# Order-2 Hyena convolution: the imaginary part of the spectrum products moved to GpSimd, VectorE's steps turned by one spectrum

## The chip, the cores and the metric

The kernel runs on one core of a Trainium2 chip. A core has five engines that run their own instruction streams and meet only at semaphores: TensorE (PE in the profile), VectorE (DVE), ScalarE (ACT), GpSimd (POOL) and SyncE (SP), which here only issues DMAs. They share an on-chip memory, SBUF, and the matmul accumulators, PSUM. The metric is the device time of one execution in microseconds.

## The reference

One layer of a diffusion backbone on 1024 tokens of width 1024, float32. The part that matters here is the Hyena branch: three streams v, x1, x2 of 512 channels, and twice a long convolution of the running stream with a filter, done as a product of spectra, followed by a gate.

```python
y = v.astype(jnp.float32)
for o, gate in enumerate((x1, x2)):
    yf = jnp.fft.rfft(y, n=2 * L, axis=1)
    y = jnp.fft.irfft(yf * kf[:, o], n=2 * L, axis=1)[:, :L] + hyena_bias[o].astype(jnp.float32) * y
    y = gate.astype(jnp.float32) * y
```

`yf * kf` is a complex product: real part xr*kr - xi*ki, imaginary part xr*ki + xi*kr. The rest of the layer (the modulated input projection, windowed attention, the merge of both branches, the routed experts) is the same in both kernels.

## The kernel before

The stages stand one after the other, each in a block of its own whose end all engines wait for: modulation and projection, attention, `hyena`, `merge`, `choice`, `experts`. `hyena` calls `spectra`, which computes the filters' spectra into `KS` (`kspec` in the profile), and then `convolve`, the function that the change touches; `merge` follows it, and its weights' loads are the first DMAs that SP issues there.

`convolve` works on four sets: two orders times two halves of 256 channels. The transforms are odd-frequency transforms of length 1024, split by the token index modulo 4 into classes, with the cosine and sine tables in `tf` and `ti`. A set's frequencies come in two chunks of 128 partitions, so there are N = 8 spectra; spectrum k is chunk k % 2 of set k // 2. For one spectrum:

- TensorE turns the set's channels by 16 transposes (`turn`, once for two spectra, L1374), ScalarE copies them to `ut` (L1434).
- TensorE does the forward transform (`forward`, L1165) in two halves, even and odd classes, into PSUM `p_j`. ScalarE copies one bank of each to `cp` (L1440), since VectorE can read the other from PSUM directly.
- VectorE, `spectral(k)`: five sums and differences of `cp` and `p_j` into `wave_a` (L1456 to L1461), two butterflies that give the spectrum, called waves here (L1468, L1469), the products with KS (L1472 to L1478), four instructions that combine frequency pairs (L1482 to L1485) and two that write the signs into `spec` (L1490, L1491). The last six are called the finish here.
- TensorE does the back transform (`back`, L1401) into PSUM `p_acc`, two chunks of a set accumulated.
- VectorE, `gating(i)`: two instructions that multiply the set's result with the gate into `ya` (L1498).

Everything between the forward and the back transform works in two buffers of 128x2x4x256, `wave_a` and `wave_b`, which each step overwrites. `ya` of set i is the input of set i+2, so `turn(2)` and `turn(3)` wait for `gating(0)` and `gating(1)`; each `turn` also waits until VectorE has read `p_j` of the spectrum before (L1458 to L1461). The order on TensorE is written out by hand: turn 0, forward 0 and 1, turn 1, forward 2, back 0, forward 3, back 1; then turn 2, forward 4, back 2, forward 5, back 3; then turn 3, forward 6, back 4, forward 7, and back 5, 6 and 7. VectorE does `spectral(0)` to `spectral(7)` in turn, with `gating(0)` behind spectrum 2, `gating(1)` behind 4, `gating(2)` behind 6 and `gating(3)` at the end. GpSimd has no instruction in this block. SP loads each set's gate rows into one of two buffers. In the expert stage, much later, GpSimd issues an indirect gather and an indirect scatter per expert (L1825, L1836), and VectorE splits the weights with a subtraction on 128x2048 (L1891).

Of the kernel before, what the change touches and what calls it, by code (L numbers as in the profile page):

```python
# [20 lines left out]
P = 128  # L21
D = 1024
L = 1024
# [1305 lines left out]
def convolve(g, KS, ti):  # L1329

    nc, sem, A = g["nc"], g["sem"], g["A"]
# [3 lines left out]
    with ExitStack() as s:  # L1335
# [3 lines left out]
        wa = sb("wave_a", [P, 2, 4, HC])  # L1339
        wb = sb("wave_b", [P, 2, 4, HC])  # L1340
        spec = sb("spec", [P, 2, 2, 2, 2, HC])
        gate = sb("gate_in", [P, 2, 2, L])
        pj = ps("p_j", [P, 2, 2, 512])
        acc = ps("p_acc", [P, 2, 4, LQ])
        gate_in = [sem(f"gate_in{i}") for i in range(2)]
# [5 lines left out]
        with nc.Block() as block:  # L1351
            @block.sync
            def _(sp):
                for i in range(SETS):
                    if i >= 2:
                        sp.wait_ge(gated, 2 * (i - 1))
                    at = HY * (i // 2 + 1) + HC * (i % 2)
                    sp.dma_start(gate[:, i % 2], g["z_dram"][at:at + HC, :].rearrange("(c p) t -> p c t", p=P))\
                      .then_inc(gate_in[i % 2], 16)
# [84 lines left out]
            def _(dve):  # L1444
                half = wa[:].rearrange("p o (a z) n -> p o a z n", z=2)
                uv = wb[:].rearrange("p u (g z) n -> p u g z n", z=2)
                steps = 0

                def spectral(k):
                    nonlocal steps  # L1450
                    i, c = divmod(k, FC)
                    KR, KI = KS[:, i, c, 0], KS[:, i, c, 1]
# [12 lines left out]
                    if k:  # L1465
                        dve.wait_ge(spec_ready, 2 * k)
                    x4 = wb[:].rearrange("p z (a b) n -> p b a z n", b=2)
                    dve.tensor_tensor(x4[:, 0], half[:, 0], half[:, 1], ALU.add).then_inc(step, 1)  # L1468
                    dve.tensor_tensor(x4[:, 1], half[:, 0], half[:, 1], ALU.subtract).then_inc(step, 1)  # L1469
                    steps += 2  # L1470
                    dve.wait_ge(step, steps)
                    dve.tensor_tensor(wa[:], wb[:], KS[:, i, c], ALU.mult).then_inc(step, 1)  # L1472
                    dve.wait_ge(step, steps + 1)
                    dve.tensor_tensor(wb[:, 0], wb[:, 0], KI, ALU.mult).then_inc(step, 1)
                    dve.tensor_tensor(wa[:, 0], wa[:, 0], wa[:, 1], ALU.subtract).then_inc(step, 1)
                    dve.tensor_tensor(wb[:, 1], wb[:, 1], KR, ALU.mult).then_inc(step, 1)
                    dve.wait_ge(step, steps + 4)
                    dve.tensor_tensor(wa[:, 1], wb[:, 0], wb[:, 1], ALU.add).then_inc(step, 1)  # L1478
                    steps += 5
                    dve.wait_ge(step, steps)  # L1480
                    y = wa[:].rearrange("p z (g h) n -> p h g z n", h=2)
                    dve.tensor_tensor(uv[:, 0], y[:, 0], y[:, 1], ALU.add).then_inc(step, 1)  # L1482
                    dve.tensor_tensor(uv[:, 1, 0], y[:, 0, 0], y[:, 1, 0], ALU.subtract).then_inc(step, 1)
                    dve.tensor_tensor(uv[:, 1, 1, 1], y[:, 0, 1, 0], y[:, 1, 1, 0], ALU.subtract).then_inc(step, 1)
                    dve.tensor_tensor(uv[:, 1, 1, 0], y[:, 0, 1, 1], y[:, 1, 1, 1], ALU.subtract).then_inc(step, 1)  # L1485
                    steps += 4
                    dve.wait_ge(step, steps)
# [5 lines left out]
                def gating(i):  # L1493
                    dve.wait_ge(b_done, FC * (i + 1))
                    s_ = i % 2
                    dve.wait_ge(gate_in[i % 2], 16 * (i // 2 + 1))
# [5 lines left out]
                for k in range(N):  # L1502
                    spectral(k)
                    if k >= 2 and k % FC == 0:
                        gating(k // FC - 1)
# [532 lines left out]
```

## Time and profile before

| what | value |
|---|---|
| device time, median of 3 runs | 2449.34 us (2447.83 to 2449.48) |
| profiled execution: its own time | 2448.38 us |
| profiled execution: span of the trace | 2446.6 us |
| TensorE busy | 2204.0 us, 90% |
| VectorE busy | 1683.9 us, 69% |
| ScalarE busy | 1106.1 us, 45% |
| GpSimd busy | 162.9 us, 7% |
| the convolution (`convolve`) | 808 to 979 us of the trace |
| in it: TensorE, VectorE, ScalarE, GpSimd busy | 133.3, 143.1, 17.7, 0.0 of 171 us |

Rows of a timeline read: start us, duration us, engine, line, operation, tile written <- tiles read, shapes, number of merged instructions, and in brackets how long the engine stood idle before and what released it. The span is from the first to the last instruction; the execution's own time has 1.8 us around it.

### The profile page before, as it was taken

How to read it: one execution, taken by the hardware profiler on the slowest of the kernel's cores; microseconds unless marked ns; L12 is line 12 of the kernel's file. 1: busy time of each engine (PE TensorE's matmuls, PEld its weight loads, DVE VectorE, ACT ScalarE, POOL GpSimd, SP SyncE). 2: the span in 40 equal slices, each digit the busy share in tenths (PEclk: the TensorE clock that was granted, in tenths of full speed). 3: DMA queues.
4: the chain of work that ended last, by engine and by line, in shares of the span. 5: the costliest groups of instructions: out<-in, count | busy, mean ns of one | idle time of the engine just before them, and what ended most of it. 6: DMA issues, size and time to landing. Idle time of an engine off the chain costs nothing. (4 is left out here: it accounts for less than half of the span.)

```text
span 2446.6 us, 26716 instructions
## 1 busy us (share of the span) xinstructions
PE 2204.0 (90%) x9902; PEld 1689.5 (69%) x9902; DVE 1683.9 (69%) x1703; ACT 1106.1 (45%) x1108; POOL 162.9 (7%) x48
## 2 busy tenths in 40 slices
PE   6699889979989787899932999999999999999998
PEld 1597678866657676344521888888888888888886
DVE  2536663237744698123468889888888889888886
ACT  3421121235610110000002877777777777777774
POOL 0000000010000000000000011111110111111100
PEclk9799989989989898899965999999999999999999
DMA  6323344230020010624242999999999999999993
GB/s 228 113 70 103 103 160 142 104 121 10 14 82 1 35 35 0 233 93 148 87 162 93 343 391 380 378 377 379 379 375 391 385 392 377 378 378 380 375 378 127
DMA packets 176025, 532.00 MB, mean 217 GB/s; under 512 B 14752, under 2 KB 52780, under 8 KB 175445
## 3 DMA queue, kind: packets, MB, share of 16 engines
q1 hardware_dynamic: 166800, 501.48, 54.7%
q0 software_dynamic: 4608, 16.78, 2.6%
q10 hardware_dynamic: 4548, 12.80, 1.3%
q8 instruction: 46, 0.75, 0.1%
q14 instruction: 23, 0.18, 0.0%
HBM read 497.47 MB, written 33.55 MB: 217 GB/s over the span
## 5 line engine op out<-in xcount | busy, mean ns | idle before, releaser
L1891 DVE TENSOR_TENSOR r_lo<-ring,r_hi 128x2048 fp32r<-128x2048 f32 x384 | 872.0, 2290 | 104.4 <-ACT r_hi L1850 103.0
L1850 ACT ACTIVATE r_hi<-ring 128x2048 fp32r<-128x2048 f32 x384 | 731.7, 1915 | 222.6 <-PE p_b L454 75.5
L452 PE MATMUL p_a<-r_hi,x_hi 128*128 128x512 f32 x512 | 203.4, 397 | 4.3 <-DVE x_lo L1902 4.3
L452 PE MATMUL p_y<-r_hi,a_hi 128*128 128x512 f32 x512 | 205.7, 402 | 0.0
L454 PE MATMUL p_y<-r_hi,a_lo 128*128 128x512 f32 x512 | 200.5, 392 | 0.0
L454 PE MATMUL p_a<-r_hi,x_lo 128*128 128x512 f32 x512 | 200.4, 391 | 0.0
L453 PE MATMUL p_a<-r_lo,x_hi 128*128 128x512 f32 x512 | 200.0, 391 | 0.0
L453 PE MATMUL p_y<-r_lo,a_hi 128*128 128x512 f32 x512 | 199.6, 390 | 0.0
L453 PE MATMUL p_b<-r_lo,x_hi 128*128 128x512 f32 x512 | 199.4, 389 | 0.0
L452 PE MATMUL p_b<-r_hi,x_hi 128*128 128x512 f32 x512 | 199.4, 389 | 0.0
L454 PE MATMUL p_b<-r_hi,x_lo 128*128 128x512 f32 x512 | 199.4, 389 | 0.0
L452 PE MATMUL p_z<-h_hi,w_hi 128*128 128x512 f32 x448 | 179.8, 401 | 0.0
L453 PE MATMUL p_z<-h_lo,w_hi 128*128 128x512 f32 x448 | 177.9, 397 | 0.0
L454 PE MATMUL p_z<-h_hi,w_lo 128*128 128x512 f32 x448 | 177.7, 397 | 0.0
L1825 POOL DMA_INDIRECT g1row<-xn_dram,idx_e x16 | 113.5, 7094 | 800.0 <-DVE idx_e L1897 795.7
L1646 ACT ACTIVATE squares<-x_new 128x1024 f32<-128x1024 f32 x8 | 8.5, 1057 | 282.6 <-DVE x_new L1683 282.6
L586 DVE TENSOR_TENSOR w_lo<-w_raw,w_hi 128x2048 fp32r<-128x2048 f32 x17 | 38.9, 2290 | 125.5 <-ACT w_hi L547 125.5
L1618 PE MATMUL p_m<-ring 128*128 128x512 f32 x256 | 111.1, 593 | 2.3 <-DVE ring L1670 2.3
L452 PEld LDWEIGHTS p_a<-r_hi,x_hi 128*128 128x128 f32 x512 | 96.6, 189 | 23.6 <-issue 4.6
L454 PEld LDWEIGHTS p_y<-r_hi,a_lo 128*128 128x128 f32 x512 | 96.1, 188 | 21.1
L454 PEld LDWEIGHTS p_a<-r_hi,x_lo 128*128 128x128 f32 x512 | 96.5, 188 | 20.6
L453 PEld LDWEIGHTS p_a<-r_lo,x_hi 128*128 128x128 f32 x512 | 96.8, 189 | 19.2
(276 smaller groups left out, 3593.7 us busy)
## 6 DMA issues: line engine op xcount, KB each, us to landing
ring<-in_w_gate SPq DMA_DIRECT2D x128, 1024.0 KB, 9.4
ring<-in_w_up SPq DMA_DIRECT2D x128, 1024.0 KB, 9.1
ring<-in_w_down SPq DMA_DIRECT2D x128, 1024.0 KB, 12.2
w_raw<-in_w_in SPq DMA_DIRECT2D x17, 1024.0 KB, 6.5
ada_rest<-in_ada_w SPq DMA_DIRECT2D x16, 1024.0 KB, 5.8
ada<-in_ada_w SPq DMA_DIRECT2D x4, 2048.0 KB, 17.2
gate_dram<-zs ACTq DMA_DIRECT2D x16, 512.0 KB, 2.7
gates_in<-gate_dram SPq DMA_DIRECT2D x16, 512.0 KB, 4.2
```

The lines of the kernel that those rows point to most:

```text
L452: pe.matmul(out, a_hi, b_hi, start=start, stop=False)
L453: pe.matmul(out, a_hi, b_lo, start=False, stop=False)
L454: return pe.matmul(out, a_lo, b_hi, start=False, stop=stop)
L586: dve.tensor_tensor(w_lo[:, u % 2], w[:, u % 2], w_hi[:, u % 2].bitcast(F32), ALU.subtract)\
L1618: mm = pe.matmul(pj[:, t % 2, h], mT[:, k, P * t:P * t + P], wo[:, k, 512 * h:512 * h + 512], start=k == 0, stop=k == KD - 1)
L1646: act.activation(junk[:], xnew[:, t % XB, :], ACT.Square, accum_out=ss[:, t:t + 1]).then_inc(sq_ready, 1)
L1825: pool.indirect_dma_start(out=xe[:], out_offset=None, in_=g["xn2_dram"][:, :], in_offset=bass.IndirectOffsetOnAxis(ap=idx_e[:, 0:1], axis=0))\
L1850: act.activation(r_hi[:, i % PARTS], ring[:, i % RAW], ACT.Copy).then_inc(hi_ready, 1)
L1891: dve.tensor_tensor(r_lo[:, i % PARTS], ring[:, i % RAW], r_hi[:, i % PARTS].bitcast(F32), ALU.subtract).then_inc(lo_ready, 1)
```

## The change

Three of VectorE's five product steps of a spectrum go to GpSimd: xr*ki (`cross`), xi*kr (`prod[:, 1]`) and their sum, the imaginary part. VectorE keeps one instruction that makes xr*kr and xi*ki, and their difference. So that the two can work at the same time, the spectrum, the products and the temporaries have buffers of their own (`wave`, `prod`, `cross`, `tmp`), and VectorE's steps are turned: the waves of spectrum k, then (at k = 3, 5, 7) a gating, the finish of spectrum k-1, and the real part of k. The next pair of waves waits for GpSimd's imaginary part, as `wave` is overwritten. The gate has one buffer instead of two. Nothing changes on TensorE and ScalarE, nor in what is computed.

```diff
--- before.py
+++ after.py
@@ -1328,6 +1328,9 @@
 
 def convolve(g, KS, ti):
 
     nc, sem, A = g["nc"], g["sem"], g["A"]
     ident, ya, tf = g["ident"], g["ya"], g["tf"]
     SETS = 2 * ORD
@@ -1336,13 +1339,17 @@
         sb, ps = g["scope"](s)
         ut = sb("ut", [P, 2, 2, 2, FC, HC])
         cp = sb("cp", [P, 2, 2, HC])
-        wa = sb("wave_a", [P, 2, 4, HC])
-        wb = sb("wave_b", [P, 2, 4, HC])
+        tmp = sb("wave_tmp", [P, 2, 4, HC])
+        wave = sb("wave", [P, 2, 4, HC])
+        prod = sb("wave_prod", [P, 3, 4, HC])
+        cross = sb("wave_cross", [P, 4, HC])
         spec = sb("spec", [P, 2, 2, 2, 2, HC])
-        gate = sb("gate_in", [P, 2, 2, L])
+        gate = sb("gate_in", [P, 2, L])
         pj = ps("p_j", [P, 2, 2, 512])
         acc = ps("p_acc", [P, 2, 4, LQ])
-        gate_in = [sem(f"gate_in{i}") for i in range(2)]
+        gate_in = sem("gate_in")
+        wave_ready, cross_ready = sem("wave_ready"), sem("cross_ready")
+        im_part, im_ready, y_read = sem("im_part"), sem("im_ready"), sem("y_read")
         t_job, x_job, b_done = sem("turn_job"), sem("x_job"), sem("back_done")
         t_ready, cp_ready, x_read = sem("ut_ready"), sem("cp_ready"), sem("x_read")
         step, spec_ready = sem("wave_step"), sem("spec_ready")
@@ -1352,11 +1359,26 @@
             @block.sync
             def _(sp):
                 for i in range(SETS):
-                    if i >= 2:
-                        sp.wait_ge(gated, 2 * (i - 1))
+                    if i:
+                        sp.wait_ge(gated, 2 * i)
                     at = HY * (i // 2 + 1) + HC * (i % 2)
-                    sp.dma_start(gate[:, i % 2], g["z_dram"][at:at + HC, :].rearrange("(c p) t -> p c t", p=P))\
-                      .then_inc(gate_in[i % 2], 16)
+                    sp.dma_start(gate[:], g["z_dram"][at:at + HC, :].rearrange("(c p) t -> p c t", p=P)).then_inc(gate_in, 16)
+            @block.gpsimd
+            def _(pool):
+                for k in range(N):
+                    i, c = divmod(k, FC)
+                    KR, KI = KS[:, i, c, 0], KS[:, i, c, 1]
+                    pool.wait_ge(wave_ready, 2 * (k + 1))
+                    if k:
+                        pool.wait_ge(im_ready, k)
+                    pool.tensor_tensor(cross[:], wave[:, 0], KI, ALU.mult).then_inc(cross_ready, 1)
+                    if k:
+                        pool.wait_ge(y_read, 4 * k)
+                    pool.tensor_tensor(prod[:, 1], wave[:, 1], KR, ALU.mult).then_inc(im_part, 1)
+                    pool.wait_ge(cross_ready, k + 1)
+                    pool.wait_ge(im_part, k + 1)
+                    pool.tensor_tensor(prod[:, 1], prod[:, 1], cross[:], ALU.add).then_inc(im_ready, 1)
 
             @block.tensor
             def _(pe):
@@ -1442,14 +1464,19 @@
 
             @block.vector
             def _(dve):
-                half = wa[:].rearrange("p o (a z) n -> p o a z n", z=2)
-                uv = wb[:].rearrange("p u (g z) n -> p u g z n", z=2)
+                half = tmp[:].rearrange("p o (a z) n -> p o a z n", z=2)
+                uv = tmp[:].rearrange("p u (g z) n -> p u g z n", z=2)
+                x4 = wave[:].rearrange("p z (a b) n -> p b a z n", b=2)
+                y = prod[:, 0:2].rearrange("p z (g h) n -> p h g z n", h=2)
                 steps = 0
 
-                def spectral(k):
+                def waves(k):
                     nonlocal steps
-                    i, c = divmod(k, FC)
-                    KR, KI = KS[:, i, c, 0], KS[:, i, c, 1]
+                    if k >= 2:
+                        dve.wait_ge(spec_ready, 2 * (k - 1))
+                    if k:
+                        dve.wait_ge(step, steps)
                     for odd in range(2):
                         dve.wait_ge(cp_ready, 2 * k + odd + 1)
                         other = pj[:, odd, 1].rearrange("p (z n) -> p z n", z=2)
@@ -1463,28 +1490,31 @@
                     dve.wait_ge(step, steps)
                     dve.wait_ge(x_read, 2 * k + 2)
                     if k:
-                        dve.wait_ge(spec_ready, 2 * k)
-                    x4 = wb[:].rearrange("p z (a b) n -> p b a z n", b=2)
-                    dve.tensor_tensor(x4[:, 0], half[:, 0], half[:, 1], ALU.add).then_inc(step, 1)
-                    dve.tensor_tensor(x4[:, 1], half[:, 0], half[:, 1], ALU.subtract).then_inc(step, 1)
+                        dve.wait_ge(im_ready, k)
+                    dve.tensor_tensor(x4[:, 0], half[:, 0], half[:, 1], ALU.add).then_inc(wave_ready, 1)
+                    dve.tensor_tensor(x4[:, 1], half[:, 0], half[:, 1], ALU.subtract).then_inc(wave_ready, 1)
+                def real_part(k):
+                    nonlocal steps
+                    i, c = divmod(k, FC)
+                    dve.wait_ge(wave_ready, 2 * (k + 1))
+                    if k:
+                        dve.wait_ge(y_read, 4 * k)
+                    dve.tensor_tensor(prod[:, 0:3:2], wave[:], KS[:, i, c], ALU.mult).then_inc(step, 1)
+                    dve.wait_ge(step, steps + 1)
+                    dve.tensor_tensor(prod[:, 0], prod[:, 0], prod[:, 2], ALU.subtract).then_inc(step, 1)
                     steps += 2
+                def finish(k):
                     dve.wait_ge(step, steps)
-                    dve.tensor_tensor(wa[:], wb[:], KS[:, i, c], ALU.mult).then_inc(step, 1)
-                    dve.wait_ge(step, steps + 1)
-                    dve.tensor_tensor(wb[:, 0], wb[:, 0], KI, ALU.mult).then_inc(step, 1)
-                    dve.tensor_tensor(wa[:, 0], wa[:, 0], wa[:, 1], ALU.subtract).then_inc(step, 1)
-                    dve.tensor_tensor(wb[:, 1], wb[:, 1], KR, ALU.mult).then_inc(step, 1)
-                    dve.wait_ge(step, steps + 4)
-                    dve.tensor_tensor(wa[:, 1], wb[:, 0], wb[:, 1], ALU.add).then_inc(step, 1)
-                    steps += 5
-                    dve.wait_ge(step, steps)
-                    y = wa[:].rearrange("p z (g h) n -> p h g z n", h=2)
-                    dve.tensor_tensor(uv[:, 0], y[:, 0], y[:, 1], ALU.add).then_inc(step, 1)
-                    dve.tensor_tensor(uv[:, 1, 0], y[:, 0, 0], y[:, 1, 0], ALU.subtract).then_inc(step, 1)
-                    dve.tensor_tensor(uv[:, 1, 1, 1], y[:, 0, 1, 0], y[:, 1, 1, 0], ALU.subtract).then_inc(step, 1)
-                    dve.tensor_tensor(uv[:, 1, 1, 0], y[:, 0, 1, 1], y[:, 1, 1, 1], ALU.subtract).then_inc(step, 1)
-                    steps += 4
-                    dve.wait_ge(step, steps)
+                    dve.wait_ge(im_ready, k + 1)
+                    dve.wait_ge(wave_ready, 2 * min(k + 2, N))
+                    dve.tensor_tensor(uv[:, 0], y[:, 0], y[:, 1], ALU.add).then_inc(y_read, 1)
+                    dve.tensor_tensor(uv[:, 1, 0], y[:, 0, 0], y[:, 1, 0], ALU.subtract).then_inc(y_read, 1)
+                    dve.tensor_tensor(uv[:, 1, 1, 1], y[:, 0, 1, 0], y[:, 1, 1, 0], ALU.subtract).then_inc(y_read, 1)
+                    dve.tensor_tensor(uv[:, 1, 1, 0], y[:, 0, 1, 1], y[:, 1, 1, 1], ALU.subtract).then_inc(y_read, 1)
+                    dve.wait_ge(y_read, 4 * (k + 1))
                     if k >= 2:
                         dve.wait_ge(b_done, k - 1)
                     dve.tensor_tensor(spec[:, k % 2, 0], uv[:, :, 0], uv[:, :, 1], ALU.add).then_inc(spec_ready, 1)
@@ -1493,16 +1523,20 @@
                 def gating(i):
                     dve.wait_ge(b_done, FC * (i + 1))
                     s_ = i % 2
-                    dve.wait_ge(gate_in[i % 2], 16 * (i // 2 + 1))
+                    dve.wait_ge(gate_in, 16 * (i + 1))
                     for j in range(2):
                         dve.tensor_tensor(ya[:, 2 * s_ + j, :].rearrange("p (n q) -> p n q", q=4),
                                           acc[:, j].rearrange("p q n -> p n q"),
-                                          gate[:, i % 2, j].rearrange("p (n q) -> p n q", q=4), ALU.mult).then_inc(gated, 1)
+                                          gate[:, j].rearrange("p (n q) -> p n q", q=4), ALU.mult).then_inc(gated, 1)
 
                 for k in range(N):
-                    spectral(k)
-                    if k >= 2 and k % FC == 0:
+                    waves(k)
+                    if k >= FC and k % FC:
                         gating(k // FC - 1)
+                    if k:
+                        finish(k - 1)
+                    real_part(k)
+                finish(N - 1)
                 gating(SETS - 1)
                 dve.wait_ge(gated, 2 * SETS)
 
```

On VectorE, the first waves of spectrum 1 (the second of eight) and what follows. Before, from L1468:

```order
L1468 TENSOR_TENSOR wave_b<-wave_a 128x2x2x256
L1469 TENSOR_TENSOR wave_b<-wave_a 128x2x2x256
L1472 TENSOR_TENSOR wave_a<-wave_b,kspec 128x2048
L1474 TENSOR_TENSOR wave_b<-wave_b,kspec 128x1024
L1475 TENSOR_TENSOR wave_a<-wave_a 128x1024
L1476 TENSOR_TENSOR wave_b<-wave_b,kspec 128x1024
L1478 TENSOR_TENSOR wave_a<-wave_b 128x1024
L1482 TENSOR_TENSOR wave_b<-wave_a 128x1024
L1483 TENSOR_TENSOR wave_b<-wave_a 128x512
L1484 TENSOR_TENSOR wave_b<-wave_a 128x256
L1485 TENSOR_TENSOR wave_b<-wave_a 128x256
L1490 TENSOR_TENSOR spec<-wave_b 128x1024
```

After the change, at the same place, from the same waves (`wave_tmp`, `wave` and `wave_prod` are the new buffers; L1513 to L1521 are the finish of spectrum 0, L1503 and L1505 the real part of spectrum 1):

```order
L1494 TENSOR_TENSOR wave<-wave_tmp 128x2x2x256
L1495 TENSOR_TENSOR wave<-wave_tmp 128x2x2x256
L1513 TENSOR_TENSOR wave_tmp<-wave_prod 128x1024
L1514 TENSOR_TENSOR wave_tmp<-wave_prod 128x512
L1515 TENSOR_TENSOR wave_tmp<-wave_prod 128x256
L1516 TENSOR_TENSOR wave_tmp<-wave_prod 128x256
L1520 TENSOR_TENSOR spec<-wave_tmp 128x1024
L1521 TENSOR_TENSOR spec<-wave_tmp 128x1024
L1503 TENSOR_TENSOR wave_prod<-wave,kspec 128x2x1024
L1505 TENSOR_TENSOR wave_prod<-wave_prod 128x1024
```

The three product steps L1474, L1476 and L1478 are gone from VectorE, and the finish now stands behind the waves of the next spectrum and ahead of the real part.

On VectorE, the first gating. Before, behind the whole of spectrum 2:

```order
L1490 TENSOR_TENSOR spec<-wave_b 128x1024
L1491 TENSOR_TENSOR spec<-wave_b 128x1024
L1498 TENSOR_TENSOR ya<-p_acc,gate_in 128x1024 x2
L1456 TENSOR_TENSOR wave_a<-cp,p_j 128x512
L1461 TENSOR_TENSOR wave_a<-cp,p_j 128x512
```

After the change, L1528 is the gating, in front of it the waves of spectrum 3, behind it the finish of spectrum 2:

```order
L1494 TENSOR_TENSOR wave<-wave_tmp 128x2x2x256
L1495 TENSOR_TENSOR wave<-wave_tmp 128x2x2x256
L1528 TENSOR_TENSOR ya<-p_acc,gate_in 128x1024 x2
L1513 TENSOR_TENSOR wave_tmp<-wave_prod 128x1024
L1514 TENSOR_TENSOR wave_tmp<-wave_prod 128x512
```

The first gating stood between spectrum 2's finish and spectrum 3's first instructions; now it stands behind spectrum 3's waves, and spectrum 2's finish has moved behind it.

On GpSimd, where the block was empty before, after the change (the first two spectra; L1375 `cross`, L1378 the other product, L1381 the sum):

```order
L1375 TENSOR_TENSOR wave_cross<-wave,kspec 128x1024
L1378 TENSOR_TENSOR wave_prod<-wave,kspec 128x1024
L1381 TENSOR_TENSOR wave_prod<-wave_prod,wave_cross 128x1024
L1375 TENSOR_TENSOR wave_cross<-wave,kspec 128x1024
L1378 TENSOR_TENSOR wave_prod<-wave,kspec 128x1024
L1381 TENSOR_TENSOR wave_prod<-wave_prod,wave_cross 128x1024
```

The same three rows stand there eight times.

## Rows read from the trace of the kernel before

**Rows 1.** The page, part 1: busy time, share of the span, instructions

```profile
PE 2204.0 (90%) x9902; PEld 1689.5 (69%) x9902; DVE 1683.9 (69%) x1703; ACT 1106.1 (45%) x1108; POOL 162.9 (7%) x48
```

**Rows 2.** Waits in 808:979: who waited for whom, us in total, times, longest

```profile
PE p_j L1374 <- DVE wave_a L1461: 18.1, 3, 10.9
DVE ya L1498 <- PE p_acc L1401: 14.1, 4, 10.0
```

**Rows 3.** VectorE timeline of spectrum 1: start us, us, instruction

```profile
836.40 0.68 DVE L1456 TENSOR_TENSOR wave_a<-cp,p_j 128x512 f32<-128x512 f32 x1
...
839.03 1.23 DVE L1468 TENSOR_TENSOR wave_b<-wave_a 128x1024 f32<-128x1024 f32 x1
...
843.75 1.23 DVE L1474 TENSOR_TENSOR wave_b<-wave_b,kspec 128x1024 f32<-128x1024 f32 x1
844.90 1.22 DVE L1475 TENSOR_TENSOR wave_a<-wave_a 128x1024 f32<-128x1024 f32 x1
846.03 1.22 DVE L1476 TENSOR_TENSOR wave_b<-wave_b,kspec 128x1024 f32<-128x1024 f32 x1
847.28 1.23 DVE L1478 TENSOR_TENSOR wave_a<-wave_b 128x1024 f32<-128x1024 f32 x1
848.54 1.23 DVE L1482 TENSOR_TENSOR wave_b<-wave_a 128x1024 f32<-128x1024 f32 x1
...
853.36 0.68 DVE L1456 TENSOR_TENSOR wave_a<-cp,p_j 128x512 f32<-128x512 f32 x1
```

**Rows 4.** Timeline around the first gating, start, us, idle before in brackets

```profile
871.98 2.36 DVE L1498 TENSOR_TENSOR ya<-p_acc,gate_in 128x1024 f32<-128x1024 f32 x2 [1.59 <-PE p_acc L1401]
874.25 0.68 DVE L1456 TENSOR_TENSOR wave_a<-cp,p_j 128x512 f32<-128x512 f32 x1
...
875.58 3.25 PE L1374 MATMUL p_j<-ident,ya 128*128 128x128 f32 x16 [3.64 <-DVE wave_a L1461]
```

**Rows 5.** Timeline, the first two VectorE instructions of the convolution

```profile
817.18 0.69 DVE L1456 TENSOR_TENSOR wave_a<-cp,p_j 128x512 f32<-128x512 f32 x1 [9.71 <-ACT cp L1440]
...
820.63 0.69 DVE L1456 TENSOR_TENSOR wave_a<-cp,p_j 128x512 f32<-128x512 f32 x1 [2.17 <-ACT cp L1440]
```

**Rows 6.** Timeline, the end of the convolution and what follows it

```profile
976.27 2.36 DVE L1498 TENSOR_TENSOR ya<-p_acc,gate_in 128x1024 f32<-128x1024 f32 x2 [10.02 <-PE p_acc L1401]
...
986.76 6.48 PE L1608 MATMUL p_m<-ya,ring 128*128 128x512 f32 x8 [10.53 <-DMA ring<-in_w_branch_a]
```

**Rows 7.** GpSimd timeline of 530:545, its only tensor arithmetic on this shape

```profile
536.50 4.68 POOL L863 TENSOR_TENSOR fpm<-fout 128x1024 f32<-128x1024 f32 x2 [5.55 <-DMA fout<-in_filt_out]
```

**Rows 8.** VectorE timeline beside it

```profile
538.74 0.69 DVE L960 TENSOR_REDUCE mx<-p_s 128x1 f32<-128x512 f32 x1 [1.32 <-PE p_s L1072]
```

**Rows 9.** Timeline of a gather beside an idle VectorE

```profile
1338.07 0.97 POOL L1825 DMA_INDIRECT g1row<-xn_dram,idx_e  x1 [13.74 <-DVE idx_e L1897]
...
1340.47 2.29 DVE L1891 TENSOR_TENSOR r_lo<-ring,r_hi 128x2048 fp32r<-128x2048 f32 x1 [3.22 <-ACT r_hi L1850]
```

**Rows 10.** Timeline of a gather beside a busy VectorE

```profile
1411.47 11.33 DVE L1891 TENSOR_TENSOR r_lo<-ring,r_hi 128x2048 fp32r<-128x2048 f32 x5
...
1413.27 7.95 POOL L1825 DMA_INDIRECT g1row<-xn_dram,idx_e  x1 [0.30 <-issue]
```

**Rows 11.** VectorE line 1891 over the whole run: duration ns min/median/max

```profile
L1891 DVE TENSOR_TENSOR r_lo<-ring,r_hi x384: 2279/2292/2296, 1324.0 to 2426.2; 128x2048 fp32r<-128x2048 f32 x192
```

**Rows 12.** GpSimd timeline at the start, a wait on its own result

```profile
1.34 0.28 POOL L286 TENSOR_SCALAR_AFFINE_SELECT ident<-ident 128x128 f32<-128x128 f32 x1 [0.25 <-POOL ones L284]
```

**Rows 13.** Timeline, TensorE restarting after the second turn, and its readers

```profile
842.54 8.68 PE L1165 MATMUL p_j<-ut,dft_in 128*128 128x256 f32 x32 [1.11 <-ACT ut L1434]
...
847.80 0.60 ACT L1440 ACTIVATE cp<-p_j 128x512 f32<-128x512 f32 x1 [5.32 <-PE p_j L1165]
...
851.26 0.60 ACT L1440 ACTIVATE cp<-p_j 128x512 f32<-128x512 f32 x1 [2.86 <-PE p_j L1165]
```

**Rows 14.** Window 842:845: busy by engine (instructions), PEclk, DMA share, GB/s

```profile
842.00:845.00 3.00, 2.46 (x6) 2.02 (x7) 2.97 (x3) 0.49 (x1) 0.00 (x0) 0.50 0.02 5
```


## The prediction

> **What bounds the kernel now.** I began with the page's busy shares: VectorE is busy 69% of the run, GpSimd 7% [rows 1]. These are averages over stages with different limits, so the stage that is changed has to be read by itself. The convolution runs from 808 to 979 us of the trace. The list of waits for that stretch says who is late: TensorE waits three times, 18.1 us in all, for VectorE's first two instructions on a spectrum before it may turn the next channels, while VectorE waits for TensorE only before the gatings [rows 2]. The timeline then shows VectorE without a gap: spectrum 1 begins at 836.40 and spectrum 2 at 853.36, so one spectrum costs it 16.96 us [rows 3]. VectorE is the bound of this stage. Its span closes as a sum: from its first instruction at 817.18 to the end of the last gating at 976.27 + 2.36 = 978.63 are 161.4 us; eight spectra are 135.7, the wait for the second copy in spectrum 0 is 2.2 [rows 5], four gatings of 874.25 - 871.98 = 2.27 are 9.1 [rows 4], the waits before the gatings are 14.1 [rows 2], of which the last is 10.0 [rows 6]. That makes 161.1. What follows cannot hide any of it: TensorE's next work waits 10.53 us for a weight whose load is issued behind this block [rows 6], so an end of the block that moves by x moves the kernel by x.
>
> **What the change takes from VectorE.** Per spectrum three instructions go to GpSimd. By their starts they occupy VectorE for 843.75 to 844.90 (1.15), 846.03 to 847.28 (1.25) and 847.28 to 848.54 (1.26), together 3.66 us [rows 3]. The subtraction of 1.13 that stays now has an instruction behind it that waits for it; the waited-for neighbours in the same rows are 0.12 longer, so the net is 3.55, and a spectrum costs VectorE 13.4 us instead of 16.96. Eight times: -28.4 us of VectorE's own time. The turning of the steps by itself costs no instruction; it puts the finish of a spectrum behind the waves of the next, and the gating between those two. The gate's single buffer costs nothing: its next load has a whole gating period, some 37 us, to land.
>
> **What it puts on GpSimd.** 24 instructions on 128x1024 f32. The trace has GpSimd do two of just this shape in 4.68 us, so 2.34 us each [rows 7], 7.0 per spectrum, 56.2 in all. If they ran beside VectorE freely, they would be covered: from the second wave of a spectrum until it needs the result for the next pair of waves, VectorE has all of its 13.4 us but that pair (2 x 1.2), 11.0 us: the finish of the previous spectrum (853.36 - 848.54 = 4.8), the first five instructions of the next (839.03 - 836.40 = 2.6), and the real part, which is the rest, 3.6 [rows 3].
>
> **Do the two run beside each other?** No row shows a VectorE instruction with two operands in SBUF beside GpSimd arithmetic, so this cost is bounded from both sides. Lower end: beside GpSimd's two additions VectorE's reductions from PSUM kept their 0.69 us [rows 8], so nothing is lost. Upper end: every GpSimd instruction excludes VectorE's SBUF-to-SBUF instructions for its whole length, and all that is not covered otherwise is added. Nearest to the case are the gathers of the expert stage, where GpSimd works beside VectorE's two-operand subtractions. The same instruction takes 0.97 us while VectorE is idle until 1340.47 [rows 9] and 7.95 us while VectorE runs five subtractions on end [rows 10]. That gather may be slowed by its queue as well, and those subtractions kept their length (2279 to 2296 ns over the whole run [rows 11]). But it says that GpSimd gets little while VectorE streams two operands. Here GpSimd is not starved for long, since VectorE stops at its own semaphores about five times per spectrum (before the waves, the product, the subtraction, the finish, the sign step), and a GpSimd instruction that has begun reads tensors for 2.34 us. So I take the upper end: the two alternate.
>
> The Trainium skill, page "SBUF — State Buffer", section "Who interferes with whom", speaks against this change: it says that VectorE with two SBUF inputs contends with a GpSimd instruction that reads SBUF, and that whichever issues first holds the shared pair for its whole instruction. By that rule the time would come out as in the sum below; by [rows 8] alone it would be the free overlap of the first rival. The gather's 0.97 against 7.95 us leans the page's way, and no run here shows the case itself.
>
> **The sum.** All on VectorE, which stays the bound:
> - 3.55 us less in each of 8 spectra: -28.4.
> - The three waits before the first gatings, 14.1 - 10.0 = 4.1 us [rows 2, 6], vanish: VectorE comes later than the back transforms: -4.1.
> - GpSimd's 24 instructions: +56.2.
> - Covered parts: the gating reads one operand from PSUM, and at three of the four gatings GpSimd's first product stands beside it: 3 x 2.27 = -6.8. In the first spectrum nothing is to be finished, and the last addition runs beside the first five instructions of the next: -2.3.
> Together +14.6. In later spectra GpSimd's three instructions are spent before VectorE reaches its PSUM reads, so nothing more is covered. A handing-over may cost extra: 0.25 us is the gap of a GpSimd wait on its own result [rows 12], and 24 times that is 6.0; I take 0 for it, since VectorE's own stop at a semaphore is 0.03 us (848.51 to 848.54, [rows 3]), and keep both ends for the range. TensorE stays below VectorE: from a turn to the next gating it needs 3.25 + 1.1 [rows 4, 13] and 871.98 - 842.54 = 29.4 us, 33.8 in all, against two spectra of 20.4. The profiled run took 2448.38 us with a span of 2446.6; 2448.4 + 14.6 = 2463.0, and the median of the three runs is 1.0 higher, so 2463.9. I say **2463.5 us**. Own range of this case: at the low end two more GpSimd instructions find cover, -4.7, at the high end the hand-overs cost 6.0: 2459 to 2470.
>
> **Rivals.**
> - *Free overlap* (faster). Then TensorE's chain becomes the bound, and three places give time. Head: the second turn of channels waits for spectrum 1's first instructions, which come 853.36 - 843.75 - 1.25 = 8.4 us earlier [rows 3]; from there to the first gating TensorE has no gap, so -8.4. Middle: a turn now follows right behind a gating, 2.4 instead of 875.58 - 871.98 = 3.6 us, at two turns: -2.4 [rows 4]. Tail: behind the third gating VectorE has 4.8 + 3.6 + 4.8 = 13.2 instead of 16.96: -3.7. Sum -14.5, so 2434.8. For it speak VectorE's unchanged 0.69 us [rows 8]; against it the gather [rows 9, 10]. GpSimd could take up to 11.0 / 3 = 3.6 us per instruction before this shrinks. It may be more: after idling 3.6 to 10.9 us TensorE restarts at the lower clock, granted 0.50 (1.2 GHz) [rows 14], and its first half transform takes 847.80 - 842.54 = 5.3 instead of 851.26 - 847.80 = 3.5 us [rows 13]. With gaps of some 2.3 us it might keep its clock: three times 1.8, down to 2429.4. No row shows such a gap. The sign turns where about two thirds of the 56.2 - 9.1 = 47.1 us land on VectorE (32.5 / 47.1).
> - *VectorE always goes first*, GpSimd gets in only while VectorE reads PSUM or stands still. Then a spectrum is 13.4 + 7.0 - 2.6 = 17.8 us: 8 x (17.8 - 16.96) = +6.7, less the 4.1 of vanished waits: +2.6, 2452. For it: the subtractions that kept their length beside the gathers [rows 11]. Against it: VectorE's stops at its semaphores, each an opening.
> - *The imaginary part arrives late although both overlap*: GpSimd slower on the spectrum's layout. It would need 5 us an instruction to cost what was saved; the 2.34 us [rows 7] are of the same shape. Small.
>
> **Chances.** Alternation 0.50 (the gather, the stops); free overlap 0.28; VectorE first 0.17; the last 0.05. The likeliest gives 2463.5. About 0.2% (4.9 us) is what a measurement here can tell from no change. Faster: 0.28 and a little of the last, 0.29. Slower: 0.50 and some of the two small ones, 0.56. Same: 0.15. As both signs hold much, the range reaches to most of the free overlap: 2432 to 2470; outside are the part of it in which TensorE also keeps its clock, and mishaps above 2470.
>
> **What the next profile would show.** Right: VectorE's instructions of 1.2 us on the waves, the finish and the signs stretched to 3 us and more, or begun late by about 2.3 us next to GpSimd's, and the PSUM readers (0.68, 0.42) unchanged; a spectrum every 20 us; no wait before the gatings; TensorE idle more than now; the block's end near 993 us. Wrong, as free overlap: every VectorE duration as now, gatings 36 us apart, GpSimd at 2.34 us, TensorE without gaps but around the gatings, the block's end near 964. Wrong, as VectorE first: VectorE's durations as now, GpSimd's product lengthened or begun late, VectorE waiting for the GpSimd addition before each pair of waves. The prediction fails if GpSimd's reads interleave with VectorE's at no loss, or if more of them than I count fall beside PSUM readers and gatings.

## The result and the profile after

The changed kernel takes 2456.62 us (median; 2454.06 to 2457.85), the kernel before in the same runs 2448.35 us. The ratio is 1.0033, 95% interval 1.0024 to 1.0042: 8.3 us slower. I had said 2463.5 us, slower, with a range of 2432 to 2470. That range holds both signs; the narrower one that I gave for alternation, 2459 to 2470, was missed by 2.4 us.

The busy shares of the changed kernel's page, part 1, beside [rows 1]:

```profile
PE 2202.3 (90%) x9902; PEld 1686.7 (69%) x9902; DVE 1696.4 (69%) x1679; ACT 1106.1 (45%) x1108; POOL 236.7 (10%) x72
```

VectorE has 24 instructions less and is busy 12.5 us longer; GpSimd's 24 instructions are busy for 73.8 us instead of the 56.2 that they would take alone. Something stretches both. The timeline of VectorE and GpSimd over spectra 2 and 3 (start us, us, engine, line, idle before in brackets) shows what; it answers to [rows 3 and 4]:

```profile
853.25 0.69 DVE L1483 TENSOR_TENSOR wave_tmp<-cp,p_j 128x512 f32<-128x512 f32 x1
...
858.33 2.35 POOL L1375 TENSOR_TENSOR wave_cross<-wave,kspec 128x1024 f32<-128x1024 f32 x1 [8.58 <-DVE wave L1495]
858.38 3.37 DVE L1513 TENSOR_TENSOR wave_tmp<-wave_prod 128x1024 f32<-128x1024 f32 x1
...
863.07 1.22 DVE L1520 TENSOR_TENSOR spec<-wave_tmp 128x1024 f32<-128x1024 f32 x1
863.11 3.38 POOL L1378 TENSOR_TENSOR wave_prod<-wave,kspec 128x1024 f32<-128x1024 f32 x1 [2.43 <-DVE wave_tmp L1516]
864.21 3.36 DVE L1521 TENSOR_TENSOR spec<-wave_tmp 128x1024 f32<-128x1024 f32 x1
...
866.63 3.14 POOL L1381 TENSOR_TENSOR wave_prod<-wave_prod,wave_cross 128x1024 f32<-128x1024 f32 x1
867.49 4.43 DVE L1503 TENSOR_TENSOR wave_prod<-wave,kspec 128x2048 f32<-128x2048 f32 x1
...
873.27 0.69 DVE L1483 TENSOR_TENSOR wave_tmp<-cp,p_j 128x512 f32<-128x512 f32 x1
...
878.19 2.35 DVE L1528 TENSOR_TENSOR ya<-p_acc,gate_in 128x1024 f32<-128x1024 f32 x2
878.35 2.35 POOL L1375 TENSOR_TENSOR wave_cross<-wave,kspec 128x1024 f32<-128x1024 f32 x1 [8.58 <-DVE wave L1495]
880.45 1.33 DVE L1513 TENSOR_TENSOR wave_tmp<-wave_prod 128x1024 f32<-128x1024 f32 x1
...
893.31 0.69 DVE L1483 TENSOR_TENSOR wave_tmp<-cp,p_j 128x512 f32<-128x512 f32 x1
```

L1513 to L1521 are the finish, L1503 and L1505 the real part, L1528 the gating; GpSimd's L1375, L1378 and L1381 are the two products and their sum. L1513 takes 1.2 us alone and 3.37 here: GpSimd's first product began 0.05 us ahead of it. L1521 takes 3.36 instead of 1.22, L1503 4.43 instead of 2.29. Each is longer by 2.14 or 2.15 us, once per GpSimd instruction, and GpSimd's second product, begun in the middle of L1520, takes 3.38 instead of 2.35: it waited for L1520 to end. Where VectorE reads PSUM nothing is stretched: the gating at 878.19 takes its 2.35 us, GpSimd's product beside it 2.35 us, and the instruction behind both only 1.33. A spectrum with a gating therefore lasts 893.31 - 873.27 = 20.04 us, as long as one without (20.02).

In the first spectrum (the same view) GpSimd came 0.05 us late, so VectorE's product kept its 2.29 us and GpSimd's took 4.45; VectorE paid 2.0 us at L1505, and then waited for the sum:

```profile
825.43 2.29 DVE L1503 TENSOR_TENSOR wave_prod<-wave,kspec 128x2048 f32<-128x2048 f32 x1
825.48 4.45 POOL L1375 TENSOR_TENSOR wave_cross<-wave,kspec 128x1024 f32<-128x1024 f32 x1 [283.00 <-DVE wave L1495]
827.76 3.25 DVE L1505 TENSOR_TENSOR wave_prod<-wave_prod 128x1024 f32<-128x1024 f32 x1
...
829.89 3.34 POOL L1378 TENSOR_TENSOR wave_prod<-wave,kspec 128x1024 f32<-128x1024 f32 x1
...
833.38 2.35 POOL L1381 TENSOR_TENSOR wave_prod<-wave_prod,wave_cross 128x1024 f32<-128x1024 f32 x1
...
835.86 1.23 DVE L1494 TENSOR_TENSOR wave<-wave_tmp 128x1024 f32<-128x1024 f32 x1 [2.28 <-POOL wave_prod L1381]
```

The end of the block, beside [rows 6]: the last back transform and the last gating.

```profile
978.31 7.17 PE L1423 MATMUL p_acc<-idft_in,spec 128*128 128x256 f32 x32 [0.87 <-DVE spec L1521]
985.52 2.36 DVE L1528 TENSOR_TENSOR ya<-p_acc,gate_in 128x1024 f32<-128x1024 f32 x2 [7.27 <-PE p_acc L1423]
```

The last wait is 7.27 us where it was 10.02. The same transform in the kernel before:

```profile
966.31 9.92 PE L1401 MATMUL p_acc<-idft_in,spec 128*128 128x256 f32 x32 [9.71 <-DVE spec L1491]
```

The beginning of that transform before, then after, in windows (us, busy us and instructions of PE, PEld, DVE, ACT, POOL, then the granted clock, the DMA share, GB/s):

```profile
966.00:970.00 4.00, 3.69 (x9) 2.94 (x10) 0.26 (x1) 0.00 (x0) 0.00 (x0) 0.50 0.00 0
```

```profile
978.00:983.00 5.00, 4.69 (x22) 4.15 (x23) 0.26 (x1) 0.00 (x0) 0.00 (x0) 1.00 0.00 0
```

The granted clock was 0.50 (1.2 GHz) after 9.7 us without matmuls and is 1.00 (2.4 GHz) now. From VectorE's first instruction (818.13) to the end of the last gating (987.88) the block takes 169.75 us, 8.3 more than the 161.45 before. That is as much as the medians differ. (The spans of the two profiled executions differ by 9.4 us, of which 0.95 lies ahead of this block.)

### The profile page after: what moved, and what is told of

Its sections match the earlier page's. It is cut to its first block and busy times, and to the rows that moved or that the text cites. A ratio compares the mean times of both kernels' runs of the same rounds, so it can differ in the third digit from the quotient of the medians.

```text
span 2456.0 us, 26753 instructions
## 1 busy us (share of the span) xinstructions
PE 2202.3 (90%) x9902; PEld 1686.7 (69%) x9902; DVE 1696.4 (69%) x1679; ACT 1106.1 (45%) x1108; POOL 236.7 (10%) x72
## 5 line engine op out<-in xcount | busy, mean ns | idle before, releaser
L1870 POOL DMA_INDIRECT out_x<-late,idx_s x16 | 42.7, 2669 | 942.9 <-DVE late L1970 942.9
```

The source lines that it names most:

```text
L1870: pool.indirect_dma_start(out=g["out"][0], in_=yo[:], in_offset=None, out_offset=bass.IndirectOffsetOnAxis(ap=idx_s[:, 0:1], axis=0), comp ...
```

## The experiments

Besides the kernel's time, each is read by the length of the block, from VectorE's first instruction to the end of its last gating: 161.45 us before, 169.75 after.

**The turned order alone.** All product steps are back on VectorE; the new buffers and the turned order stay.

```diff
-                    pool.tensor_tensor(cross[:], wave[:, 0], KI, ALU.mult).then_inc(cross_ready, 1)
...
+                    dve.tensor_tensor(cross[:], wave[:, 0], KI, ALU.mult).then_inc(cross_ready, 1)
+                    dve.tensor_tensor(prod[:, 1], wave[:, 1], KR, ALU.mult).then_inc(im_part, 1)
+                    dve.tensor_tensor(prod[:, 1], prod[:, 1], cross[:], ALU.add).then_inc(im_ready, 1)
```

> The turned order and the separate buffers of the change are kept, but all five product steps stand on VectorE and GpSimd does nothing in this block. Theory (exclusion: a GpSimd instruction and a VectorE instruction with two SBUF operands shut each other out for their whole length): no VectorE instruction is stretched, a spectrum costs VectorE 17.0 us as before the change, and only the three short waits before the gatings (4.1 us) vanish, so 3 to 5 us faster than the kernel before, 2444 to 2446 us. Rival (the turned order with its extra waits is what costs, not the two engines side by side): as slow as the changed kernel, 2455 us or more.

2440.79 us, ratio 0.9972 (0.9961 to 0.9982); the block takes 153.2 us. The turned order is not what costs; it gains 7 us, more than the 3 to 5 that I expected. Its timeline from one gating to the next:

```profile
871.02 2.35 DVE L1527 TENSOR_TENSOR ya<-p_acc,gate_in 128x1024 f32<-128x1024 f32 x2
...
906.81 2.35 DVE L1527 TENSOR_TENSOR ya<-p_acc,gate_in 128x1024 f32<-128x1024 f32 x2
```

35.8 us instead of some 37.5, and no wait for TensorE before them. The block is 8.3 us shorter: 4.1 are the vanished waits, 2.8 the last wait, which fell to 7.26 and which I had left out, and some 1.4 are short gaps between VectorE's instructions ((35.8 - 2.3) / 2 = 16.75 us per spectrum instead of 16.96). So moving the three steps to GpSimd, on top of the turned order, cost 2456.6 - 2440.8 = 15.8 us.

**GpSimd writes only.** Its three instructions are memsets of 128x1024; the imaginary part is left out.

```diff
-                    pool.tensor_tensor(cross[:], wave[:, 0], KI, ALU.mult).then_inc(cross_ready, 1)
+                    pool.memset(cross[:], 0.0).then_inc(cross_ready, 1)
```

> The changed kernel with GpSimd's three instructions per spectrum replaced by memsets that write 128x1024 values and read nothing; the imaginary part is left out of the computation. VectorE's instructions, all waits and their order are those of the changed kernel. Theory (exclusion of reads): every VectorE instruction keeps the length it has alone (1.22 and 2.29 us), gatings come about 36 us apart and bound by TensorE, and the time is that of my free-overlap rival, 12 to 19 us below the kernel before, 2429 to 2437 us. Rival A (any GpSimd access to SBUF stalls VectorE): the same three VectorE instructions are stretched by nearly the length of a memset, about 1 us each, 24 us in all. Rival B (the order costs): no faster than the kernel before.

2426.05 us, ratio 0.9909 (0.9893 to 0.9926); the block takes 138.3 us. GpSimd's and VectorE's instructions around one finish:

```profile
878.14 0.95 POOL L1375 MEMSET wave_cross<- 128x1024 f32 x1 [10.65 <-DVE wave L1495]
878.22 1.23 DVE L1513 TENSOR_TENSOR wave_tmp<-wave_prod 128x1024 f32<-128x1024 f32 x1
...
881.85 0.95 POOL L1381 MEMSET wave_cross<- 128x1024 f32 x1
881.89 1.22 DVE L1521 TENSOR_TENSOR spec<-wave_tmp 128x1024 f32<-128x1024 f32 x1
```

Each VectorE instruction has its own length beside a running memset. Same instructions and waits on VectorE, 30.6 us less than the changed kernel, and 3 us below the 2429 that I gave as the bottom. TensorE's rows behind the third turn say more:

```profile
896.88 3.42 PE L1396 MATMUL p_j<-ident,ya 128*128 128x128 f32 x16 [2.54 <-DVE ya L1528]
...
901.41 7.17 PE L1165 MATMUL p_j<-ut,dft_in 128*128 128x256 f32 x32 [1.11 <-ACT ut L1456]
```

The forward transform behind a turn takes 7.17 us, at all three turns, where it took 8.68 to 8.79 before [rows 13]; the granted clock is 1.00 from 901.4 to 905 us, where the beginning of the same transform before (917.4 to 921 us) has 0.54. With gaps of 2.54 us ahead of the turns TensorE kept its clock at the first two (2.49 and 2.17 us long) and lost it only for a part of the third (granted 0.66 from 895 to 900 us). I had allowed for that at the bottom of the range. A memset takes 0.95 us and not 2.35, so this run isn't the free overlap of the real work.

**GpSimd reads one tensor.** Its instructions multiply by a constant; the imaginary part is not computed.

```diff
-                    pool.tensor_tensor(cross[:], wave[:, 0], KI, ALU.mult).then_inc(cross_ready, 1)
+                    pool.tensor_scalar(cross[:], wave[:, 0], 0.5, None, ALU.mult).then_inc(cross_ready, 1)
```

> The changed kernel with GpSimd's three instructions replaced by multiplications with a constant, which read one tensor of 128x1024 and write one; the imaginary part is not computed. Theory (exclusion for the length of whatever instruction reads): the same VectorE instructions are stretched as in the changed kernel, each by the length of the GpSimd instruction less about 0.2 us; if that instruction takes 1.1 to 1.3 us alone, by 0.9 to 1.1 us. Rival (only the second operand of a two-operand GpSimd instruction collides): no stretching, times as in the write-only run.

2437.35 us (one run); block 150.0 us.

```profile
891.91 3.80 POOL L1378 TENSOR_SCALAR wave_prod<-wave 128x1024 f32<-128x1024 f32 x1 [0.70 <-DVE wave_tmp L1516]
893.00 2.06 DVE L1521 TENSOR_TENSOR spec<-wave_tmp 128x1024 f32<-128x1024 f32 x1
...
904.40 2.77 POOL L1375 TENSOR_SCALAR wave_cross<-wave 128x1024 f32<-128x1024 f32 x1 [4.52 <-DVE wave L1495]
904.64 1.22 DVE L1528 TENSOR_TENSOR ya<-p_acc,gate_in 128x1024 f32<-128x1024 f32 x1 [0.32 <-PE p_acc L1423]
```

The first two rows are the finish of one spectrum, the last two stand at a gating. Beside the gating such an instruction takes 2.77 us; I take that for its length alone. VectorE's L1521 is longer by 0.84 us (2.06), not by 2.77 less 0.2: my expectation of the size was wrong, and so was the rival, since there is a collision. VectorE is shut out for a part of the GpSimd instruction only.

**Half the elements.** The changed kernel with 128x512 on GpSimd; half of the imaginary part stays zero.

```diff
-                    pool.tensor_tensor(prod[:, 1], wave[:, 1], KR, ALU.mult).then_inc(im_part, 1)
+                    pool.tensor_tensor(prod[:, 1, 0:2], wave[:, 1, 0:2], KR[:, 0:2], ALU.mult).then_inc(im_part, 1)
```

> The changed kernel with GpSimd's three instructions cut to half their elements (128x512); half of the imaginary part is left at zero. Theory (VectorE is shut out while GpSimd reads, in proportion to the elements): the three stretched VectorE instructions of a spectrum are each 1.0 to 1.2 us longer than alone instead of 2.15. Rival (a fixed price for each change of owner): still about 2 us each.

2435.20 us (one run); block 148.1 us.

```profile
890.57 2.31 POOL L1380 TENSOR_TENSOR wave_prod<-wave,kspec 128x512 f32<-128x512 f32 x1 [2.43 <-DVE wave_tmp L1518]
891.66 2.29 DVE L1523 TENSOR_TENSOR spec<-wave_tmp 128x1024 f32<-128x1024 f32 x1
...
893.02 2.06 POOL L1383 TENSOR_TENSOR wave_prod<-wave_prod,wave_cross 128x512 f32<-128x512 f32 x1
893.88 3.35 DVE L1505 TENSOR_TENSOR wave_prod<-wave,kspec 128x2048 f32<-128x2048 f32 x1
```

L1523 (the finish's last) is 2.29 - 1.22 = 1.07 and L1505 (the product) 3.35 - 2.29 = 1.06 us longer: half of 2.15, as expected. So the price goes with the elements, and no fixed price of changing owner is seen.

**GpSimd starts late.** It waits until VectorE has done the real part.

```diff
                     pool.wait_ge(wave_ready, 2 * (k + 1))
+                    pool.wait_ge(step, 5 * (k + 1))
```

> The changed kernel, but GpSimd starts on a spectrum only when VectorE has finished its real part, so that the first of its three instructions falls beside VectorE's five instructions that read PSUM, and VectorE then waits for the other two. Theory: GpSimd's instructions take 2.35 us each, no VectorE instruction with a PSUM operand is stretched, and VectorE waits some 4.5 to 5 us before each pair of waves: a spectrum of about 18.2 us, a block some 2 us shorter than in the changed kernel and 4 to 6 us longer than before, 2452 to 2455 us. Rival (the engines share smoothly and what matters is only that both work): slower than the changed kernel, since it has less overlap, 2460 us or more.

2456.51 us, ratio 1.0033 (1.0020 to 1.0045); block 169.2 us. The rows of one spectrum:

```profile
893.16 1.23 DVE L1495 TENSOR_TENSOR wave<-wave_tmp 128x1024 f32<-128x1024 f32 x1 [1.82 <-POOL wave_prod L1382]
...
904.10 0.69 DVE L1484 TENSOR_TENSOR wave_tmp<-cp,p_j 128x512 f32<-128x512 f32 x1
904.14 2.36 POOL L1376 TENSOR_TENSOR wave_cross<-wave,kspec 128x1024 f32<-128x1024 f32 x1 [11.11 <-DVE wave_prod L1506]
...
911.42 1.23 DVE L1495 TENSOR_TENSOR wave<-wave_tmp 128x1024 f32<-128x1024 f32 x1 [4.78 <-POOL wave_prod L1382]
```

The mechanism is as expected: PSUM readers and GpSimd undisturbed side by side, a wait of 4.78 us before the waves, 18.26 us per spectrum. The time is not: the last spectrum has no next one to cover anything, VectorE waits 7.4 us there, TensorE idles 5.6 us and its last transform takes 9.1 us; I had expected 2452 to 2455 us. Overlap with collisions costs as much as letting VectorE wait for GpSimd.

**Only what PSUM readers cover.** First the sum alone on GpSimd, behind VectorE's last product:

```diff
-                    pool.wait_ge(wave_ready, 2 * (k + 1))
...
                     pool.wait_ge(cross_ready, k + 1)
                     pool.wait_ge(im_part, k + 1)
                     pool.tensor_tensor(prod[:, 1], prod[:, 1], cross[:], ALU.add).then_inc(im_ready, 1)
```

> The turned order with both cross products on VectorE and only their sum on GpSimd, issued behind VectorE's last product, so that it falls beside VectorE's five instructions that read PSUM (2.6 us). Theory (two-operand instructions in SBUF exclude each other, PSUM readers do not): no VectorE instruction is stretched, GpSimd's sum takes 2.35 us and is over before the next waves, a spectrum costs VectorE 15.6 us instead of 16.9 with everything on VectorE; since TensorE is nearly the bound in the middle, 3 to 7 us below the turned order with all products on VectorE, 2434 to 2438 us. Rival (any work of GpSimd costs VectorE as much as it saves): 2440 us or more, with VectorE instructions stretched or late.

2438.04 us, ratio 0.9954 (0.9940 to 0.9967), in the block 149.2 us. GpSimd's sum beside VectorE's PSUM readers:

```profile
896.21 1.22 DVE L1503 TENSOR_TENSOR wave_prod<-wave,kspec 128x1024 f32<-128x1024 f32 x1
897.34 0.68 DVE L1476 TENSOR_TENSOR wave_tmp<-cp,p_j 128x512 f32<-128x512 f32 x1
897.57 2.37 POOL L1374 TENSOR_TENSOR wave_prod<-wave_prod,wave_cross 128x1024 f32<-128x1024 f32 x1 [14.43 <-DVE wave_prod L1503]
...
900.07 1.22 DVE L1487 TENSOR_TENSOR wave<-wave_tmp 128x1024 f32<-128x1024 f32 x1 [0.19 <-POOL wave_prod L1374]
```

No VectorE instruction of the block is stretched. The waves come 0.19 us late, as the sum ends 0.1 us behind the readers. Before two of the gatings VectorE now waits 0.65 us for TensorE, so TensorE begins to bound the middle, and 2438.04 us is at the upper end of what I expected. Then one product in addition, beside the gatings, and the last sum back on VectorE:

```diff
+                    if k >= FC and k % FC:
+                        pool.wait_ge(wave_ready, 2 * (k + 1))
+                        pool.wait_ge(im_ready, k)
+                        pool.tensor_tensor(cross[:], wave[:, 0], KI, ALU.mult).then_inc(cross_ready, 1)
+                    if k < N - 1:
```

> As the run with only the sum on GpSimd, and in addition GpSimd makes one cross product beside the gatings, at spectra 3, 5 and 7, where VectorE reads PSUM for 2.3 us; the last spectrum's sum stays on VectorE, since nothing would cover it there. Theory: the one product collides with VectorE by 0.1 us only, VectorE saves another 3 x 1.1 us and the tail 1.2 us; TensorE's chain of 34 to 35 us from gating to gating lets through at most part of it: 1 to 4 us below the run with only the sum, 2431 to 2436 us. Rival (collisions come back because GpSimd's product begins late): no gain, and VectorE's first finish instruction behind each gating stretched by 1 us or more.

2433.76 us, ratio 0.9939 (0.9926 to 0.9953), block 146.9 us: 15 to 16 us faster than the kernel before, and the fastest here that computes the layer. The product beside the first gating costs VectorE 0.11 us, at L1521, the first of the finish here, and beside the other two nothing:

```profile
865.76 2.35 DVE L1536 TENSOR_TENSOR ya<-p_acc,gate_in 128x1024 f32<-128x1024 f32 x2
865.92 2.35 POOL L1375 TENSOR_TENSOR wave_cross<-wave,kspec 128x1024 f32<-128x1024 f32 x1 [2.57 <-DVE wave L1493]
868.02 1.33 DVE L1521 TENSOR_TENSOR wave_tmp<-wave_prod 128x1024 f32<-128x1024 f32 x1
```

**The last back transform.** The kernel before, with matmuls whose results nobody uses between its last two back transforms.

```diff
                 back(6)
+                pe.wait_ge(x_read, 2 * N)
+                for _ in range(20):
+                    class_sum(pe, pj[:, 0, 0, 0:HC], tf[:, 0], ut[:, 1, 0, 0], 0)
                 back(7)
```

> The kernel before, with 40 matmuls more on TensorE between its last two back transforms, where it stands idle for 9.7 us; their results are not used. This tests the term of my sum that left the last wait for TensorE at 10.0 us, while it was 7.3 us in the changed kernel. Theory (the last back transform took 9.9 us because TensorE had stood idle and restarted at the lower clock): it takes 7.2 us, the last wait 7.3 us, and the kernel is 2.8 us faster than before, 2445 to 2446 us. Rival (the transform waits for something else at the end): unchanged.

2452.84 us, ratio 1.0017 (1.0007 to 1.0026), slower where I expected faster: the additional matmuls ran 17.4 us and held the transform up, but it then took 7.07 us. With half of them:

> The kernel before with the additional matmuls between its last two back transforms cut from 40 to 20. The run with 40 kept TensorE busy for 17.4 us and so held the last back transform up by 7 us, though that then took 7.07 us. 20 should take 8.6 us, from about 956 to 965 us, and end just before the last spectrum is ready at about 966. Theory (the lower clock after standing idle is what made the last back transform 9.9 us long): it starts when its spectrum is ready, takes 7.1 to 7.2 us, the last wait of VectorE is 7.3 us instead of 10.0, and the block is 2.7 us shorter, 2446 to 2447 us. Rival: the block keeps its 161.4 us.

2445.18 us, ratio 0.9988 (0.9978 to 0.9997), block 159.1 us:

```profile
955.52 8.80 PE L1165 MATMUL p_j<-ut,dft_in 128*128 128x256 f32 x40
...
965.39 7.17 PE L1401 MATMUL p_acc<-idft_in,spec 128*128 128x256 f32 x32 [1.07 <-DVE spec L1494]
972.60 2.36 DVE L1501 TENSOR_TENSOR ya<-p_acc,gate_in 128x1024 f32<-128x1024 f32 x2 [7.27 <-PE p_acc L1401]
```

With `range(10)` the loop makes 20 matmuls instead of 40; an f32 matmul leaves two records here, so the row has x40, as the back transform's 16 have x32. The transform starts when its spectrum is ready and takes 7.17 us instead of 9.92, the wait is 7.27. The block is 2.35 us shorter, where I expected 2.7.

## Why the prediction held, and which of its sizes were off

**The mechanism** was right: GpSimd's instructions that read SBUF and VectorE's instructions with two SBUF operands exclude each other, those that read PSUM are free. The prediction had little to go by: its one VectorE row beside GpSimd arithmetic [rows 8] reads PSUM and so says nothing of the case, and whether the gather's 7.95 us [rows 10] had this cause isn't tested. The write-only run shows that the reads do it, with VectorE's program unchanged, and the turned order by itself is excluded as a cause: it gains. The signs came as said, a spectrum every 20.02 us and no wait before the first three gatings; the block ends at 987.9 us and not near 993. The rule cited from the Trainium skill ("SBUF — State Buffer", "Who interferes with whom") held in direction and in its exceptions for PSUM readers and for a GpSimd instruction that only writes. That whoever comes first holds the pair for its whole instruction did not hold: a one-operand instruction of 2.77 us shut VectorE out for 0.84.

**How GpSimd gets in** was half right. I had it enter where VectorE stops at its semaphores. L1521 (864.21) follows L1520 without a wait and still gave way to GpSimd's second product, which had begun at 863.11: the one that asked first goes first. VectorE first, my second rival, is out by that.

**The sum.** Term by term, measured in the changed kernel's trace:

- VectorE's own work: -28.4 predicted. The block without the rest (169.75 less 2.2 for the second copy, 9.1 for the gatings, 7.3 for the last wait and 43.3, see below: 107.9) is 13.49 per spectrum: -27.8. This term is a remainder. From start to start a spectrum is 20.02 - 3 x 2.15 = 13.57, as in the write-only run (841.35 to 854.92), and 0.2 less where a gating hides VectorE's stop before the finish.
- The three short waits: -4.1, and none is left: -4.1.
- GpSimd's share on VectorE: +56.2 - 6.8 - 2.3 = +47.1 predicted. Measured: four spectra of 3 x 2.15, three with a gating of 0.11 + 2 x 2.15, and in the first 2.03 at L1505 and the wait of 2.28 for the sum: +43.3. At the gatings the covered places were as said. In the first spectrum GpSimd's second product stood beside the PSUM readers, and not its sum, for which VectorE waited; that cost 4.3 against 4.7 in my sum. The price of one of the 18 other collisions was 2.15 and not 2.34, since VectorE is shut out for less than the whole instruction.
- The last wait: I left it at 10.0 us. It was 7.3: -2.7. In the turned order the last but one back transform runs later, TensorE stood idle for 0.87 us instead of 9.71, and the last one ran at a granted clock of 1.00 instead of 0.50 in its beginning. The run with the shorter filling shows the same 2.7 us in the kernel before.

Together +8.7, with 8.3 measured; the 0.4 are what my sum of the block before (161.1 us) lacked of its 161.45. So of the 6.3 us by which I was too high 3.8 are GpSimd's share, nearly all of it the length of one exclusion, and 2.7 the clock of one transform. No price of the hand-overs shows in the rows, as taken. The sign came with a forecast of +14.6 us for 8.3 measured, both misses on the same side.

**Free overlap** was priced too low as well: the block without collisions takes 138.3 us, 23.2 less than before, where I had 14.5, or 19.9 with the clock kept. By TensorE's rows the head gave 8.3 us and the middle 2.2, as priced. The kept clock gave 6.8 (4.7 in the three forward transforms, 2.1 in the three turns together) instead of 5.4. The tail gave 5.9 instead of 3.7, of which 2.1 are the last wait (7.90 instead of 10.02). How much of this a free overlap of the real work would have given isn't measured.

## What to carry to other kernels

Where VectorE is the bound, moving a two-operand step from it to GpSimd paid here only if GpSimd's instruction stood beside VectorE instructions that read PSUM, not beside those that read two tensors in SBUF: a step of 1.2 us moved cost 2.15 us beside the latter, and 0.2 us at most beside the former. Count the covered time first (here 2.6 us per spectrum and 2.3 per gating) and move only as much as fits. And look at what reordering alone gives: of the 15.7 us of the best version some 7 come from the turned order without GpSimd.

## What the runs showed of the hardware that I had not expected

- VectorE is shut out for less than GpSimd's instruction: 2.15 of 2.35 us for two operands of 128x1024, 1.07 of 1.27 for two of 128x512 (both times all but 0.2), 0.84 of 2.77 for one of 128x1024. A memset of 0.95 us does not shut it out at all.
- The exclusion also stretches GpSimd: its first product took 4.45 us when VectorE's 2.29 us product had begun 0.05 us earlier.
- TensorE's last back transform: 9.92 us after 9.7 us idle, 9.09 after 5.6, 7.17 after 0.87 or 1.07, and 7.17 also after 3.78 in the run with only the sum on GpSimd. Filling an idle stretch with 20 unused matmuls brought 3.5 us (2448.64 us for the kernel before in the same runs, 2445.18), at the edge of what the measurement tells.
